# A run of 24 extra matmuls on TensorE between the first prefix transposes and the k projections of a hybrid retention block

## The reference, cut to what matters

```python
u = rmsnorm(x, norm1_w) * (1 + sc1) + sh1          # sc1, sh1 = silu(c) @ w_ada + b_ada
q, k, v, og, cb, cc, cx, ga, gb = split(u @ w_in)
ret = head_groupnorm(retention(rotary(q), rotary(k) * 128 ** -0.5, v), ret_gn_w)
y_ret = (silu(og) * ret) @ w_ret_out
y_conv = (cb * causal_conv(cc * cx, conv_w)) @ w_conv_out
h = x + g1 * ((sigmoid(ga) * y_ret + sigmoid(gb) * y_conv) @ w_o)
h = h + g2 * (relu((rmsnorm(h, norm2_w) * (1 + sc2) + sh2) @ w_ff1) ** 2 @ w_ff2)
out = rmsnorm(h, final_norm_w)
```

## Time and profile before

| what | us |
|---|---|
| three runs of the program, median (lowest to highest) | 1316.8 (1314.06 to 1318.7) |
| the profiled execution's own time | 1309.52 |
| its span on the slowest core (core 7) | 1308.1 |
| spans of the 8 cores | 1297.1 to 1308.1 |
| busy on core 7: TensorE matmul | 1222.8 (93%) |
| busy on core 7: VectorE / ScalarE / GpSimd | 513.1 / 437.1 / 485.8 |

### The profile page before, as it was taken

How to read it: one execution, slowest core, us unless ns; L and a number is a source line. 1 busy time by engine, 2 the same in 40 slices (tenths; PEclk the granted TensorE clock), 3 DMA queues, 4 the chain that set the end, 5 groups by cost and what they waited for, 6 DMA issues and landing times.

```text
span 1308.1 us, 19081 instructions; the slowest of 8 cores (1297.1 to 1308.1 us)
## 1 busy us (share of the span) xinstructions
PE 1222.8 (93%) x6320; PEld 580.6 (44%) x6320; DVE 513.1 (39%) x951; ACT 437.1 (33%) x738; POOL 485.8 (37%) x501
## 2 busy tenths in 40 slices
PE   2578899999999999999899999999999999999997
PEld 0243344444444455555444444454444444444443
DVE  5455455677422157777308333420000450000145
ACT  2354444222211137777532222343320113331011
POOL 1267100000000058888564222256640136663012
PEclk9789899999999999999999999999999999999999
DMA  9968900385664040000574222994545549846233
GB/s 168 189 181 180 159 7 1 46 127 87 98 96 65 8 74 2 1 2 1 88 125 111 97 97 81 172 207 74 89 73 76 119 138 184 129 65 93 45 90 128
DMA packets 86016, 123.30 MB, mean 94 GB/s; under 512 B 4640, under 2 KB 69152, under 8 KB 85920
## 3 DMA queue, kind: packets, MB, share of 16 engines
q0 software_dynamic: 67632, 70.26, 37.8%
q1 hardware_dynamic: 15984, 43.43, 10.4%
q10 hardware_dynamic: 2304, 8.39, 1.6%
HBM read 175.54 MB, written 16.78 MB: 147 GB/s over the span
## 4 chain that ended last, share of the span: by engine, by line
PE 86%; DMA 5%; DVE 2%; ACT 2%; issue 2%; POOL 1%; SPq 1%; DVEq 0%; POOLq 0%; ACTq 0%
PE PS L306 84%; DMA ring<-w_in 4%; PE PS L477 1%; DMA scr<-x_main 1%; SPq L238 1%; ACT X L485 1%; PE PS L1018 0%; DVE AR L980 0%; ACT Z L485 0%; DVE scr L437 0%; POOL Z L1118 0%; ACT scr L1004 0%; PE PS L945 0%; PE PS L942 0%; POOL ring L238 0%
## 5 line engine op out<-in xcount | busy, mean ns | idle before, releaser
L306 PE MATMUL PS<-X,ring 128*128 128x512 bf16 x2560 | 570.7, 380 | 10.8 <-ACT scr L1042 6.5
L306 PEld LDWEIGHTS PS<-X,ring 128*128 128x128 bf16 x2560 | 249.7, 98 | 310.8 <-issue 17.7
L306 PE MATMUL PS<-ring,Z 128*128 128x512 bf16 x896 | 207.5, 386 | 11.2 <-DMA ring<-w_in 7.1
L306 PEld LDWEIGHTS PS<-ring,Z 128*128 128x128 bf16 x896 | 88.2, 99 | 119.3 <-issue 21.4
L1281 DVE TENSOR_TENSOR AR<-PS,G_t 128x512 f32<-128x512 f32 x16 | 11.1, 692 | 294.5 <-PE PS L306 294.5
L1262 ACT ACTIVATE scr<-PS 128x512 f32<-128x512 f32 x128 | 76.3, 597 | 140.4 <-PE PS L306 89.1
L306 PE MATMUL PS<-Y,ring 128*128 128x512 bf16 x512 | 120.0, 379 | 0.0
L306 PE MATMUL PS<-ring,X 128*128 128x512 bf16 x512 | 117.8, 379 | 1.8 <-DVE AR L980 1.8
L306 PE MATMUL PS<-ring,Y 128*128 128x512 bf16 x512 | 113.4, 379 | 0.0
L1265 POOL TENSOR_TENSOR Z<-scr 128x512 bf16<-128x512 f32 x64 | 67.1, 1053 | 37.8 <-ACT scr L1262 33.2
L1265 POOL TENSOR_TENSOR Y<-scr 128x512 bf16<-128x512 f32 x64 | 66.6, 1041 | 36.8 <-ACT scr L1262 30.9
(11 more groups left out here) (167 smaller groups left out, 1342.5 us busy)
## 6 DMA issues: line engine op xcount, KB each, us to landing
ring<-w_ff POOLq DMA_DIRECT2D x32, 1024.0 KB, 8.9
ring<-w_in POOLq DMA_DIRECT2D x17, 1024.0 KB, 16.3
scr<-x_main SPq DMA_DIRECT2D x25, 512.0 KB, 6.5
ring<-w_ada POOLq DMA_DIRECT2D x12, 1024.0 KB, 12.4
scr<-h1s SPq DMA_DIRECT2D x32, 256.0 KB, 5.3
y<-scr ACTq DMA_DIRECT2D x16, 512.0 KB, 4.6
h1s<-scr SPq DMA_DIRECT2D x12, 512.0 KB, 5.3
scr<-x_pre SPq DMA_DIRECT2D x8, 512.0 KB, 16.3
```

The costliest lines, as they stand in the source:

```text
L306: S.op("pe", lambda e: e.matmul(out, lhsT, rhs, start=start, stop=stop), reads=list(lkeys) + list(rkeys), writes=[okey])
```

## The change

Behind the transposes of the first group, 24 matmuls are put on TensorE. Each has the all-ones tile `ones_bf` as weights, streams the first four `crep` tiles (512 columns, bf16), and writes all of bank 2 with `start` and `stop` both true. Nothing reads what they write: bank 2 is next written by the transposes of the second group, which stand behind them on the same engine. They read and write nothing else, and no other engine gets an instruction more or less.

```diff
         for kp in range(4):
             p_tpart(0, kp, 4 + kp, "act" if kp % 2 == 0 else "dve")
+        for _ in range(24):
+            mm(pa[2], ("pa", 2), ones_bf[:, :], ["ones"], crep[:, 0:4, :].rearrange("p k m -> p (k m)"), [("crep", k) for k in range(4)], True, True)
         pair_do(0)
         pair_do(1)
```

## The result

In the first comparison the changed kernel took 1307.02 us (median of four runs, 1306.55 to 1307.65) against 1316.8 us for the kernel before (the three runs shown above): a ratio of 0.9926, 95% interval 0.99 to 0.9953. In some executions the cores of a die show a lower granted clock and the time is some per cent longer; these are left out of every median and ratio here.

A forecast was written before the change was run, and what follows sets the result against it. TensorE was taken to bound nine tenths of the kernel, with the slowest core's prefix stage setting the time before a constant rest. The hidden fill's 1.7 us clock gain gave 1316.8 - 1.7 = 1315.1 us, range 1310.5 to 1318.8.

The forecast's parts named there:

- The base of the sum: Starting time for the forecast: the 1316.8 us median of the runs, from which 1.7 us was taken.
- The mechanism: The fill keeps TensorE busy before the k projections, so they start at clock 1.00 instead of 0.50: 1.7 us less.
- the bound of 0.3%: Whole kernel: a measurement can tell about 0.3%, 3.95 us, from no change; staying within it got 0.73.
- The fill hides in the wait: TensorE before the k projections: 24 matmuls take 5.34 us inside a 7.13 us wait for the k columns.
- The clock stays at 1.00, 1.7 us less: First k projection on TensorE: at clock 1.00 it takes 1.89 us instead of 3.59.
- the forecast's 1.8 us: TensorE idle time left between the fill's end and the k columns' landing, claimed short enough to keep clock 1.00.
- The shift is carried to 147 us and the end: From the first k projection onward: the full 1.7 us reaches 147 us and is then carried one to one.
- The sentence that the rotation of tile 0 starts 1.7 us earlier: VectorE after the first k projection: tile 0's rotation and GpSimd's three operations on it start 1.7 us earlier.
- 1160.8 and 1160.7 us: From the first matmul behind L678 to the span's end, on cores 7 and 1: taken as a constant.
- The rule on transposes: At the fill: transposes don't count as activity for the full clock, so the fill could run slow, ending at 1318.3 us; chance 0.08.
- the estimate of 8.8 us: First group's 32 transposes: their time by the skill's figure of about 275 ns each, leaving no gap to fill.
- The bigger rival: x_main loads on the last cores meet weight transfers like core 1's: 5.5 us less in all, 1311.3 us; chance 0.20.

The follow-up runs named there:

- fill8: The change with 8 extra matmuls instead of 24, against the kernel before: 1309.80 us, ratio 0.9993.
- thin24: The change with its 24 extra matmuls of 16 columns instead of 512, against the kernel before: 1311.45 us, ratio 1.0003.
- r24: The change itself timed again, in alternation with the kernel before: 1308.89 us, ratio 0.9984.
- multi: The change plus 24 extra matmuls ahead of the second group's transposes and 12 ahead of the third's, against the kernel before: 1304.95 us, ratio 0.997.
- late32: A first fill of 32 matmuls and the third in-loop weight load at tile 14 instead of 10, against the kernel before: 1302.60 us, ratio 0.996.
- fill32: The change with 32 extra matmuls instead of 24, against the kernel before: 1309.77 us, ratio 0.999.
- late0: No fill, only the third in-loop weight load at tile 14 instead of 10, against the kernel before: 1305.08 us, ratio 0.9975.

## Why the prediction was wrong

**The base of the sum failed. The mechanism held, at about half its size.** The prediction noted that the profiled execution was 7.3 us below the median of the runs shown, and then took "against the median: 1316.8 - 1.7". Its other sum, "against the profiled execution: 1309.5 - 1.7 = 1307.8", is 0.8 us from the 1307.02 that was measured. In four later sets of runs, each on one chip, the kernel before had medians of 1311.20, 1308.69, 1308.73 and 1308.30 us. Of its 85 runs there one (1314.2 us) reached 1314.06 us, the lowest of the three runs shown. Three runs within 4.6 us of each other looked like a base; the profiled execution, outside them, was the better witness. That its sum came so close is luck in part: the changed kernel's later medians are 1308.89, 1308.54 and 1307.88 us, and the 1.7 us in the sum isn't what the change is worth.

The change's own worth, from the three ratios measured beside many runs of the kernel before, is 0.9984, 0.9997 and 0.9999: a mean of 0.9993, 0.9 us, of which only the first is just clear of 1; the kernel before against itself gave 1.0005. By the bound of 0.3% it is no change that can be told, which the prediction had at 0.73. Averaged over the cores instead of taking the slowest, the spans of the changed kernel are 0.8, 1.4 and 2.0 us shorter in the three later sets. Why the first comparison's runs of the kernel before had a median 5.6 to 8.5 us above the later ones stays open: no trace of those runs exists, and it isn't known what chip they were on. The 0.9926 was not reproduced in three tries.

Step by step:

1. *The fill hides in the wait.* Right. It takes 5.34 us (5.13 where the record of one matmul is missing) and ends before the k columns on all eight cores (gaps of 1.02 to 3.52 us in the first trace of the change).
2. *The clock stays at 1.00, 1.7 us less.* Right where the gap was short, and the size per core is right: A to B of 11.6 to 11.7 us on the best cores against 13.3. Missized as a value for all cores. Averaged over the 64 cores of the eight traces whose only fill is the 24, it is 12.29 us, and 13.25 over the five without a full fill (fill8 and thin24 among them): 0.96 us. The rest went two ways. The gap is no constant 1.8 us, because the transposes end 2 to 3 us apart on different cores: 23 of the 64 cores began the projections below 1.00, and their mean is 12.93 us. No core with a gap under 2.08 us was among them, and every one with more than 2.64 us was; from 2.08 to 2.64 us, 13 kept 1.00 and 7 did not. The gap of 2.55 us that left the clock at 1.00 in the earlier trace rows was thus one outcome of two, while the forecast's 1.8 us was safe.
3. *The shift is carried to 147 us and the end.* Missized, in three places. The sentence that the rotation of tile 0 starts 1.7 us earlier overlooked the variance ahead of it on VectorE: on 21 of the 41 cores that began at 1.00 it held the rotation (to 2.08 up to 3.85 us behind the start of the projections), and their mean A to B is 12.19 us against 11.65 for the other 20. Core 7's own rows, shown above, had it: the rotation waited 1.44 us for TensorE, so it could come no more than 1.44 us forward while the variance stayed. Then, A to C keeps 1.3 us on average (59.6 without, 58.3 with the fill), but the kernel's time is that of the slowest core, and this is picked by larger differences: the clock behind the wait near 81 us, and the wait on x_main (C to D, 27 to 37 us). A core that gains 1.7 us is seldom the one that ends last. And the rest behind D is no constant. The prediction read 1160.8 and 1160.7 us from two cores; over the 144 cores of all traces it is 1156.8 to 1164.9. The granted clock is a part of that: the 69 cores with a mean of 1.00 behind D need 1159.6 us on average, the 75 with 0.99 need 1161.8. What else is in it stays open. In r24, core 0 is at D 2.4 us before core 5 and ends 2.0 us behind it (D at 141.38 and 143.75, spans of 1306.3 and 1304.3 us).
4. *The rule on transposes.* The rule of the Trainium skill's "TensorE: Matmul & The Clock Gate", section "Part 4: PE-mode transpose", could have put the fill at the low clock. It did not happen: on core 0, behind 1.95 us of transposes, 23 matmuls of the fill took 5.13 us, the high clock's time, and no first fill of 24 or 32 in any trace (104 cores) took longer than at that clock. That doesn't refute the rule, since gaps of up to 2.02 us with nothing at all on TensorE didn't cost the clock either. Whether transposes alone could raise the clock is shown by no run here. What the trace refutes is the estimate of 8.8 us and not the section's 275 ns: a single transpose has a record of 0.27 us at 81.80 and of 0.22 us at 78.75 in multi, near that figure, but 32 in a row overlap and take 1.95 us.
5. *The bigger rival.* It named the right resource, the x_main loads beside the weight transfers, and was refuted as a consequence of this change: C to D is 30.69 us on average after it and 31.04 before, its longest value 34.21 and 35.35. It took moving the weight load (0.9975 without any fill) to get it. The prediction's argument that load and transfer move together with the chain fits: on core 7 tile 12's projection (C) and the issue of the third weight load of the loop both come 2.1 us earlier behind A (59.45 and 54.92 us before, 57.35 and 52.81 after).

The version with all three (fills at three places, the weight load at tile 14, the third transposes behind 16 matmuls) beats both kernels: 0.9929 with a first fill of 24 and 0.9933 with 32, on two chips, 8.8 and 8.7 us less than the kernel before.

## What to carry to other kernels

Take the base of a forecast from as many runs as there are, and where the profiled execution disagrees with three timed runs, widen the range to hold both. When a kernel's time is that of its slowest core, look for what makes one core slow (here a weight load that meets the activations' loads, and a clock that falls in a 3 us wait) before speeding up what all cores share; a gain ahead of a load-bound wait can be given back there, so move the load as well. Before a gain is passed on to the next engine, look at what else stands ahead of the reader there and when it ends. Extra matmuls in a wait keep the clock only if they reach close to its end on every core; here 2 us was close enough and 3 was not.

## What the runs showed of the hardware that was not expected

The granted clock's cost came in two sizes. In the 14 us around the wait near 81 us all eight cores of late32 show 0.76 or 0.88, though the wait itself is 2.98 or 2.99 us on every one of them, as on core 7 of the kernel before. Over the fifteen traces without the later fills 119 of 120 cores show one of the two values (the other, on a core of fill32, is 0.79). So two cores with the same program and the same wait differ by 3.4 us at half clock, and which size a core gets changed from core to core and between traces. Nor did the length of a gap alone decide: with 24 matmuls ahead, cores with gaps of 2.08 to 2.64 us began the next matmuls at 1.00 in 13 cases and lower in 7. And a weight transfer of 1 MB, as it lands in bf16, issued 14 us later (121.45 instead of 107.43) took 1.5 to 3.9 us off the mean stretch with the x_main loads (31.04 and 33.42 in two traces of the kernel before, 29.50 in late0) and brought its spread between cores from 7 us to 1.5.
